# Splitting each weight of the first group by one operation of 1024 columns per engine instead of two of 512

## What is computed

```
proj = rmsnorm(h) @ w_in                         # per head: k, v, q and the gate z
qkv  = silu(conv4(proj[..., :GDN_QKV_W]))        # causal depthwise convolution, 4 taps
tmat = eye + strict_lower(beta * (k k^T) * decay)
u, w = triangular_solve(tmat, [v*beta, k*beta*exp(g)])
for each chunk:  v_new = u - w @ S;  o = q_dec @ S + qk @ v_new;  S = S*d + k_dec^T @ v_new
h = h + (rmsnorm(o) * silu(z)) @ w_out
```

## Time and profile before

| what | us |
|---|---|
| median of the three timed runs | 2708.56 |
| profiled execution | 2697.99 |
| its span | 2696.2 |
| TensorE busy | 2446.4 (91%) |
| VectorE busy | 1644.2 (61%) |
| ScalarE busy | 1018.5 (38%) |
| GpSimd busy | 608.8 (23%) |

### The profile page before, as it was taken

How to read it: one execution, slowest core, us unless ns; L and a number is a source line. 1 busy time by engine, 2 the same in 40 slices (tenths; PEclk the granted TensorE clock), 3 DMA queues, 4 the chain that set the end, 5 groups by cost and what they waited for, 6 DMA issues and landing times. The chain is left out here.

```text
span 2696.2 us, 42354 instructions
## 1 busy us (share of the span) xinstructions
PE 2446.4 (91%) x14889; PEld 2030.7 (75%) x14889; DVE 1644.2 (61%) x3955; ACT 1018.5 (38%) x3069; POOL 608.8 (23%) x941
## 2 busy tenths in 40 slices
PE   5478888889999999999999599999998999999997
PEld 4467777768888888888887378878886777777775
DVE  4367777767777777777777223333334667666674
ACT  4244554543333333333333245433333233333332
POOL 0043333312221222122212022100001233323331
PEclk8789999999999999999999599999998999999998
DMA  6765454335544555444442267643456222222221
GB/s 188 204 214 172 158 181 166 119 118 166 188 147 136 163 182 165 136 150 152 147 148 89 69 213 255 228 161 139 168 205 269 79 79 71 89 72 79 71 72 49
DMA packets 274323, 394.71 MB, mean 146 GB/s; under 512 B 80066, under 2 KB 188178, under 8 KB 273714
## 3 DMA queue, kind: packets, MB, share of 16 engines
q1 hardware_dynamic: 241314, 370.85, 41.0%
q10 hardware_dynamic: 32800, 21.17, 2.7%
HBM read 268.56 MB, written 123.95 MB: 146 GB/s over the span
## 5 line engine op out<-in xcount | busy, mean ns | idle before, releaser
L1361 PE MATMUL p_psp<-xg,p_whi 128*128 128x512 f32 x1536 | 531.6, 412 | 0.0
L1361 PE MATMUL p_psp<-xg,p_wlo 128*128 128x512 f32 x768 | 317.4, 413 | 0.0
L1361 PEld LDWEIGHTS p_psp<-xg,p_whi 128*128 128x128 f32 x1536 | 280.2, 190 | 42.6
L1056 DVE SCALAR_TENSOR_TENSOR p_acc<-p_proj,p_taps,p_acc 128x512 f32<-128x512 f32 (+1 forms) x288 | 238.7, 829 | 5.5
L1383 PE MATMUL p_psp<-xg,p_whi 128*128 128x264 f32 x1024 | 218.4, 302 | 24.8 <-POOL p_wlo L1304 17.2
L2008 PE MATMUL first_q<-first_w,p_o 128*128 128x512 f32 (+1 forms) x864 | 206.0, 397 | 15.6 <-DVE first_w L1972 15.6
L2554 PE MATMUL first_q<-first_w,p_hT 128*128 128x512 f32 x720 | 194.5, 410 | 11.0 <-DMA p_hT<-hT_dram 11.0
L2008 PEld LDWEIGHTS first_q<-first_w,p_o 128*128 128x128 f32 (+1 forms) x864 | 156.7, 183 | 58.2 <-issue 13.6
L2554 PE MATMUL p_pso<-p_wo,p_oT 128*128 128x512 f32 x768 | 193.3, 402 | 7.9 <-DVE p_oT L2465 4.2
L1383 PEld LDWEIGHTS p_psp<-xg,p_whi 128*128 128x128 f32 x1024 | 166.7, 195 | 27.5 <-issue 26.6
L2008 PE MATMUL p_psz<-p_wk,p_o 128*128 128x512 f32 x768 | 181.3, 392 | 0.0
(11 more groups left out here) (295 smaller groups left out, 5009.3 us busy)
## 6 DMA issues: line engine op xcount, KB each, us to landing
p_whi<-w_dram SPq DMA_DIRECT2D x92, 512.0 KB, 4.3
p_wlo<-w_dram SPq DMA_DIRECT2D x92, 512.0 KB, 5.5
raw<-w_a_in SPq DMA_DIRECT2D x36, 512.0 KB, 6.1
w_dram<-p_whi SPq DMA_DIRECT2D x34, 512.0 KB, 3.8
w_dram<-p_wlo SPq DMA_DIRECT2D x34, 512.0 KB, 5.3
p_o<-hT_dram SPq DMA_DIRECT2D x34, 512.0 KB, 4.7
hT_dram<-p_hT SPq DMA_DIRECT2D x32, 512.0 KB, 3.4
p_hT<-hT_dram SPq DMA_DIRECT2D x30, 512.0 KB, 4.4
```

The source lines that it names most:

```text
L1056: nc.vector.scalar_tensor_tensor(a, p[:, c + part:part + GW], w, a, ALU.mult, ALU.add).then_inc(conv_done if part == 3 and it >= H else ta ...
L1361: ins = nc.tensor.matmul(ps_p[f % 2][:], (w_hi, w_lo)[i][:, f, kc * P:(kc + 1) * P], xg[:, g % 2, j, kc, META:GW], start=r == 0, stop=r == ...
```

## The change

`split_high` and `split_low` lose the argument `part` and take all 1024 columns in one operation, which counts both halves on its semaphore. In the steps, ScalarE does the whole weight in the slot of the first half, and GpSimd in the slot of the second.

```
-            def split_high(it, f, part, first=False):
+            def split_high(it, f, first=False):
...
-                cols = slice(part * D // 2, (part + 1) * D // 2)
-                if part == 0:
-                    if not (first and f < 2):
-                        act.wait_ge(w_in[slot], 16 * ((NF // 2) * it + f // 2))
...
-                nc.scalar.activation(w_hi[:, f, cols], w_raw[:, slot, cols], ACT.Copy).then_inc(hi_ready, 1)
+                nc.scalar.activation(w_hi[:, f, :], w_raw[:, slot, :], ACT.Copy).then_inc(hi_ready, 2)
...
                     for item, f, part in slot.split:
-                        split_high(item, f, part)
+                        if part == 0:
+                            split_high(item, f)
...
-            def split_low(it, f, part):
+            def split_low(it, f):
-                cols = slice(part * D // 2, (part + 1) * D // 2)
-                pool.wait_ge(hi_ready, 2 * (NF * it + f) + (part + 1))
-                nc.gpsimd.tensor_tensor(w_lo[:, f, cols], w_raw[:, f % 2, cols], w_hi[:, f, cols].bitcast(f32),
-                                        ALU.subtract).then_inc(lo_ready, 1)
+                pool.wait_ge(hi_ready, 2 * (NF * it + f) + 2)
+                nc.gpsimd.tensor_tensor(w_lo[:, f, :], w_raw[:, f % 2, :], w_hi[:, f, :].bitcast(f32),
+                                        ALU.subtract).then_inc(lo_ready, 2)
...
                     for item, f, part in slot.split:
-                        split_low(item, f, part)
+                        if part:
+                            split_low(item, f)
```

More of the change, by code:

```diff
@@ L871, in link @@
                 act.wait_ge(act_chain, links[0])
-            def split_high(it, f, part, first=False):
+            def split_high(it, f, first=False):
                 slot = f % 2
-                cols = slice(part * D // 2, (part + 1) * D // 2)
-                if part == 0:
-                    if not (first and f < 2):
-                        act.wait_ge(w_in[slot], 16 * ((NF // 2) * it + f // 2))
-                    if not first:
-                        act.wait_ge(proj_ps, 2 * NF * (it - 1) + (2 * f + 2))
-                        act.wait_ge(w_out[f], 32 * it)
-                nc.scalar.activation(w_hi[:, f, cols], w_raw[:, slot, cols], ACT.Copy).then_inc(hi_ready, 1)
+                if not (first and f < 2):
+                    act.wait_ge(w_in[slot], 16 * ((NF // 2) * it + f // 2))
+                if not first:
+                    act.wait_ge(proj_ps, 2 * NF * (it - 1) + (2 * f + 2))
+                    act.wait_ge(w_out[f], 32 * it)
+                nc.scalar.activation(w_hi[:, f, :], w_raw[:, slot, :], ACT.Copy).then_inc(hi_ready, 2)
             def evacuate(it, u):
@@ L1024, in _ @@
             for f in range(NF - 1):
-                for part in range(2):
-                    split_high(0, f, part, True)
+                split_high(0, f, True)
             act.wait_ge(cleared, 1)
@@ L1339, in step @@
                     for item, f, part in slot.split:
-                        split_low(item, f, part)
+                        if part:
+                            split_low(item, f)
             pool.wait_ge(cleared, 1)
             for f in range(NF - 1):
-                for part in range(2):
-                    split_low(0, f, part)
+                split_low(0, f)
             run(pool, step)
```

## The result

Four runs of the changed kernel took 2735.58 to 2741.89 us, median 2737.95; four of the kernel before, on the same chip, had a median of 2708.26. The ratio is 1.0129, with a 95% interval of 1.0115 to 1.0142; it isn't the ratio of the two medians, by which the change costs 29.7 us, or 1.1%. The forecast was 2730.5, in a range of 2713 to 2746. The profiled execution took 2735.58 us (span 2733.8), 37.6 more than the one of before (2697.99), against 21.9 by the sum. From L883 on the code stands two lines higher than before, from L1304 on three.

A forecast was written before the change was run, and what follows sets the result against it. VectorE, taking turns with GpSimd, was held to delay TensorE's hand-ordered work; 3.35 us in each of six steps (20.1) plus 1.8 gave 21.9 us, taking the median from 2708.56 to 2730.5, range 2713 to 2746.

The forecast's parts named there:

- the sum: Delays at three places in six steps, 20.1 us, plus 1.8 us for the second step: 21.9 us together.
- the turns by whole instructions: VectorE and GpSimd exclude each other for one whole instruction, so a 1024-column split keeps VectorE out twice as long.
- Durations: A whole weight takes GpSimd 2.37 us and ScalarE 1.05 us; the removed instructions count for nothing.
- the rival in which the turn is given up: GpSimd yields inside a long operation, or VectorE's delay is made good: 2708.6 or 2715.6 us; chance 0.11.
- the faster case: VectorE gets through during long splits and the removed second half frees it at 477: down to 2703.8 us; chance 0.07.
- place two: At 456.8 to 461.7 of a step, the split delays the four-column copy and update of X by 1.09 us.
- Place one: At 438 to 448, two weights back to back delay the clamp before the sigmoid by 1.17 us per step.
- the second walk: At 438 to 448, VectorE's 40x225 product goes ahead of GpSimd's split: 0.67 us late instead of 1.17.
- the clock rival: TensorE also drops to 1.2 GHz after longer stops: 7.6 to 15.2 us more, up to 2746; chance 0.16.
- place three: At 469.2 to 475, the split delays VectorE's multiply-add and the subtraction TensorE stops for at 475.07 by 1.09 us.
- The opening: The opening and first step cost nothing: GpSimd's first weight ends about 0.2 us later, but longer waits follow.
- The second step: It has place one and place three without most of place two; put at 1.8 us.

The follow-up runs named there:

- the late version: Changed kernel with ScalarE's whole split issued where the second half stood, not the first; 2705.59 us, ratio 1.0018 to the kernel before.
- the first run: Kernel before, with ScalarE splitting a whole weight at once and GpSimd keeping two 512-column halves, both after the whole high part; 2718.46 us, ratio 1.0073.
- the stops filled: Changed kernel with 9, 20 and 16 unread identity transposes put into TensorE's three longest stops per step; 2719.79 us, ratio 1.0067 to the kernel before.
- the quarters: Kernel before, with each GpSimd half cut in two, four 256-column operations per weight, ScalarE unchanged; 2704.09 us, ratio 1.0001.

## Why the prediction came out as it did

The forecast's direction, its places and their stops held, and of its mechanism the turns by whole instructions. The total was 7.4 us low by the median, inside the range. Part of that closeness is luck: the turns were put too high and the clock at nothing, two misses that point opposite ways.

*Durations.* A whole split of GpSimd was put at 2.37 us: 2.36 to 2.38 where VectorE leaves it alone (the late version). *The turn through a long operation.* No row of before was longer than 512 columns. The 40x256 copy of 2.04 us and the four-column copy of 1.67 show that 1024 columns keep VectorE out to their end, so the rival in which the turn is given up is out, and with it the faster case, which was to be decided by the copy of place two staying near 0.60.

*Place one* was put at 1.17 us with GpSimd's split ahead of the product by 0.07, or 0.67 were the product first by a hair. The product was first. From its start to the clamp's it is 9.67 us (461.94 to 471.61), and 8.98 in the earlier trace rows: 0.69 late, the second walk. The estimate chose the wrong side of a tie, 0.5 us per step too much. The stop for the state, which the clock rival put at 3.0, is 2.38 for the same reason.

*Place two* was put at 1.09 and measured 1.07, *place three* 1.09 and 1.11; the stops were to be 1.5 and 2.9 and are 1.44 and 2.92. The prediction put both down to the longer turn. That is right at place two and not needed at place three. In the kernel before, the second halves of these two places and the update of X were:

```profile
460.42 1.28 POOL L1304 TENSOR_TENSOR p_wlo<-raw,p_whi 128x512 fp32r<-128x512 f32 x1 [1.00 <-ACT p_whi L883]
...
475.28 1.29 POOL L1304 TENSOR_TENSOR p_wlo<-raw,p_whi 128x512 fp32r<-128x512 f32 x1 [4.13 <-ACT p_whi L883]
...
461.23 0.41 DVE L1194 TENSOR_TENSOR p_X<-p_X,p_psl 128x256 f32<-128x256 f32 x1
```

At place two the second half began ahead of the update of X already. What the merge made longer is the one turn that the four-column copy waits out, and in the first run, with two turns there, the stop is 0.34. At place three the second half stood behind r (475.07), and the merge brought it ahead; two separate halves pay the same there. What the prediction didn't ask is what a later place would do: the late version pays nothing at either place with whole splits.

*The opening* need not cost anything, as said: the second profiled execution starts the first step 0.04 us earlier than the kernel before, the first one 2.1 later. The first step itself lost 1.1 to 1.3, which the sum had at zero; why is not shown.

*The clock* is the term that was left out of the sum. It was a rival of its own (0.16), at 7.6 to 15.2 us on top, and the forecast took the case without it because only one step of six was counted as having lost time that way. The trace of before has a second one, the last, from 506.68 to 558.58 us, at a granted clock of 0.93. In the changed kernel all seven lost some, at granted clocks of 0.88 to 0.97. The parts come out of the step lengths. The last six of the seven steps take 307.3 us before, 335.1 after, and 320.8 with the stops filled and the clock at 1.00; six at 50.76 would be 304.6, an estimate that takes the last step, which has fewer matmuls, as long as the others. So the turns cost 320.8 - 304.6 = 16.2, the clock took 335.1 - 320.8 = 14.3 after and 2.7 before, 11.6 more, and 27.8 in all. The second step went from 52.41 to 55.13, and to 54.67 with the stops filled: 2.3 by the turns, where the sum had 1.8, and 0.5 by the clock. Turns 18.5 against the 21.9 of the sum, 3.0 of the difference from the tie at place one (six times 0.5); clock 12.1 against none. The rival was right beside the forecast, not in its place. These sizes rest on one profiled execution each, and on the filled stops costing TensorE nothing themselves.

Not settled: why VectorE had the first turn at 461.94, when GpSimd's split starts 0.01 us earlier in the record. No run tells more. The Trainium skill, page "SBUF — State Buffer", section "Who interferes with whom", says of VectorE in a two-port mode and GpSimd: "Whoever issues first gets the shared pair for the whole instruction". The second half of that is what the copy's 2.04 us shows, and the multiply-add, with two inputs in SBUF, does the same with its 2.75; the first half can't be read from starts so close together.

## What to carry to other kernels

Where two engines take turns, ask of each operation which operand the other engine still owes at that moment, and how long the turn is that it must wait out. Ahead of the operand both count: here two halves cost 15 us and one whole 30. Behind it even the whole costs little. Merging two operations is a change of schedule besides: it moves the second one's work to the first one's place, or the first one's to the second's, and here the first cost 30 us and the second 5. Cutting the pieces is no sure gain: the quarters took a microsecond of waiting off a step, and the slower clock took it back. Where a change lengthens TensorE's stops, the slower clock behind them belongs into the sum, sized by a step of the trace that already shows it.

## What the runs showed of the hardware that was not expected

A stop of TensorE cost more than its own length: 14.7 us in seven steps went away when 45 products without use per step filled three stops. The products did nothing for the operands that TensorE waits for; all that they changed is that it worked meanwhile, and the granted clock of the stretch rose from 0.92 to 1.00. This isn't so for each stop: in four steps of the first run that follow each other the stop for r is 2.89 or 2.90 us, and their granted clocks are 0.97, 1.00, 0.97 and 1.00.

GpSimd's operation has little fixed cost: two of 512 columns back to back took 2.54 us undisturbed, one of 1024 took 2.37. What merging saves on that engine is 0.17 us.
